# Output products and means of the linear attention, one step of the softmax later

## Chip, cores and metric

The kernel runs on one core of a Trainium2 chip. The metric is the device time of one execution in microseconds (us), lower is better; 3 runs of the kernel before are given.

## What is computed

One layer of a hybrid decoder: a SwiGLU block (FFN), a mixer, a second SwiGLU block, for 512 tokens of width 1024 in float32. The mixer has two branches. The first is a causal softmax attention with forget gates, 8 heads of width 64, whose queries come in blocks of 128. The second is a gated linear attention, 4 heads in chunks of 64 tokens:

```python
attn = where(tril, q_in @ k_in.T, 0)      # inside a chunk
state[n+1] = decay[n] * state[n] + k_st[n].T @ v[n]
o = attn @ v + q_in @ state               # "o" below
o = o * rsqrt(mean(o*o) + eps) * gain     # the mean is "ms" below
```

Then both branches are projected, gated, summed and projected once more.

## The kernel before

All engines run hand-written programs in a fixed order, joined by semaphores. A float32 product is made of three matmuls on high and low parts (lines 1601 to 1609), so TensorE (PE) has most of the work.

The part around the change is a loop over 38 steps, sl = 0 to 37, which each engine writes out in its own order: ScalarE (ACT) from line 905, VectorE (DVE) from 1472, TensorE from 1863. Steps 0 to 31 each start one softmax block: head sl // 4, query block sl % 4, so that its width is 128, 256, 384 or 512 keys for sl % 4 = 0 to 3. In one step:

- TensorE makes the scores of block sl (lines 1876 to 1878) after a wait for the exponentials of block sl - 2 (its count is sl - 1, line 1869). It then runs some blocks of input projection that fill the step (line 1883, called "filling" here): 3, 3, 2 and 0 blocks of three matmuls for sl % 4 = 0 to 3 from step 16 on (line 324). Then come the pieces of the linear attention that `gla_slots` gives to the step, then the transposes of the probabilities of block sl - 2 (line 1949), and in each fourth step, sl % 4 = 3, the product with the values of one head (line 1959).
- DVE takes the maximum of block sl (line 1476), the reciprocal of its sum (1480), work on a finished filling unit, the low part of the transposed probabilities of block sl - 2 (1494), in some steps sums of a head (1500) or the low part of a pair of heads (1505), and then the linear attention's pieces: the chain of states (1516, 1519), a gated product (1538), the scaled output (1543) and the low part of the squares (1545). Last, in some steps, the low part of a weight unit (1041).
- ACT takes the exponentials of block sl (912), the high part of the transposed probabilities (940), a sum of a head (946) or a pair's high part (950), the linear attention's copies and squares (968, 971, 975, 978), and the scaling of the probabilities (981).

The pieces of the linear attention are numbered: 0 and 1 transposes of keys, 2 and 3 the chunk scores of heads 0 and 1, 4 and 5 the key-value products of this pair ("kv"; piece 5 also holds DVE's chain of seven states), 6 the output product o of head 0, 7 its mean ms, 8 and 9 the same of head 1; 10 to 17 repeat 2 to 9 for heads 2 and 3. An ms product waits for the high and low parts of the squares (line 1938), which ACT (line 975) and DVE (line 1545) make of the output product in the step in which that product stands. Each piece alternates between two PSUM banks and waits for the reader of the piece two before it (line 1899).

```python
if sl >= 2:
    pe.wait_ge(exp_done, sl - 1)
...
if kind == "ms":
    pe.wait_ge(sq_lo_out, n + 1)
    mm(dst, mean_g[:, :], sq_hi, start=True, stop=False)
```

After the loop ACT makes the logarithm and the exponential of all means (lines 991 and 993, step 36), DVE and ACT finish the branch's output, and TensorE goes on with the gate projections (line 1968).

Of the kernel before, what the change touches and what calls it, by code (L numbers as in the profile page):

```python
# [108 lines left out]
def macaron_layer(nc, h_store, x_t, g1cols, x, w1g, w1u, w1d, g1post, gmpre, w_in, b_forget, w_alpha, b_alpha,  # L109
                  gla_g, w_bf, w_bg, w_out, gmpost, g2pre, w2g, w2u, w2d, g2post, out):  # L110
    with ExitStack() as ctx:
# [200 lines left out]
        def gain(g):  # L312
            return g.rearrange("(o n) -> o n", o=1).to_broadcast([P, D])


        gla_slots = {14: (0,), 16: (1,), 17: (2, 3), 18: (4, 5), 20: (6,), 22: (7, 8), 24: (9, 10), 25: (11, 12),
                     26: (13,), 28: (14,), 30: (15, 16), 32: (17,)}
        gated_slots = {25: 0, 29: 1, 33: 2, 37: 3}
        SLOTS_B = NS + 6

# [1816 lines left out]
```

## Time and profile before

| | us |
|---|---|
| median of 3 runs | 1080.15 |
| lowest, highest | 1079.99, 1081.3 |
| the profiled execution | 1081.57 |
| its span, first to last instruction | 1079.8 |
| its TensorE busy | 1067.4 |
| its VectorE, ScalarE busy | 721.7, 528.1 |

The mean granted clock of TensorE was 0.999 of full speed. Times in the trace are microseconds from the start of the span. A row of the timeline gives start, duration, engine, line, operation, operands and count of merged instructions; in square brackets stands how long the engine sat idle before and what released it. A matmul's duration includes the pipeline's latency, so successive matmuls overlap in it: the distance from one start to the next is what one costs.

### The profile page before, as it was taken

How to read it: one execution, taken by the hardware profiler on the slowest of the kernel's cores; microseconds unless marked ns; L12 is line 12 of the kernel's file. 1: busy time of each engine (PE TensorE's matmuls, PEld its weight loads, DVE VectorE, ACT ScalarE, POOL GpSimd, SP SyncE). 2: the span in 40 equal slices, each digit the busy share in tenths (PEclk: the TensorE clock that was granted, in tenths of full speed). 3: DMA queues.
4: the chain of work that ended last, by engine and by line, in shares of the span. 5: the costliest groups of instructions: out<-in, count | busy, mean ns of one | idle time of the engine just before them, and what ended most of it. 6: DMA issues, size and time to landing. Idle time of an engine off the chain costs nothing.

```text
span 1079.8 us, 16040 instructions
## 1 busy us (share of the span) xinstructions
PE 1067.4 (99%) x6490; PEld 951.6 (88%) x6490; DVE 721.7 (67%) x870; ACT 528.1 (49%) x765; POOL 44.6 (4%) x96
## 2 busy tenths in 40 slices
PE   8999999999999999999999999999999999999997
PEld 6899999998888978888888888889899999998886
DVE  6788998889535663476664333458778888789334
ACT  7354555557324573667773222344445455466222
POOL 2000000000001210001000000011000000000001
PEclk9999999999999999999999999999999999999999
DMA  9522422421721544333115335315524224313512
GB/s 301 186 79 79 150 86 79 155 81 40 260 79 54 176 124 108 84 78 80 40 40 156 97 97 172 100 39 176 156 79 149 87 79 154 121 39 105 207 39 79
DMA packets 118134, 121.20 MB, mean 112 GB/s; under 512 B 6544, under 2 KB 100768, under 8 KB 118064
## 3 DMA queue, kind: packets, MB, share of 16 engines
q1 hardware_dynamic: 113744, 113.37, 33.8%
q10 hardware_dynamic: 3344, 4.20, 1.4%
q0 software_dynamic: 976, 2.66, 0.7%
q8 instruction: 48, 0.79, 0.3%
q14 instruction: 22, 0.18, 0.1%
HBM read 111.80 MB, written 6.29 MB: 109 GB/s over the span
## 4 chain that ended last, share of the span: by engine, by line
PE 91%; DVE 3%; ACT 3%; issue 1%; DMA 1%; POOL 0%; ACTq 0%; DVEq 0%; POOLq 0%
PE bank L1616 17%; PE bank L1702 11%; PE bank L1704 11%; PE bank L1703 11%; PE bank L1606 7%; PE bank L1608 7%; PE bank L1607 7%; PE bank L1764 2%; PE bank L1765 2%; PE bank L1766 2%; PE bank L1852 1%; PE bank L1853 1%; PE bank L1854 1%; PE bank L1671 1%; PE bank L1672 1%
## 5 line engine op out<-in xcount | busy, mean ns | idle before, releaser
L1702 PE MATMUL bank<-tc,w_hi 128*128 128x256 f32 x576 | 163.0, 283 | 0.0
L1703 PE MATMUL bank<-tc,w_hi 128*128 128x256 f32 x576 | 163.0, 283 | 0.0
L1704 PE MATMUL bank<-tc,w_lo 128*128 128x256 f32 x576 | 163.0, 283 | 0.0
L1041 DVE TENSOR_TENSOR w_lo<-raw,w_hi 128x1024 fp32r<-128x1024 f32 x71 | 86.6, 1221 | 96.4 <-ACT w_hi L603 96.3
L1606 PE MATMUL bank<-u_hi,w_hi 128*128 128x512 f32 x312 | 123.9, 397 | 0.2 <-issue 0.2
L1702 PE MATMUL bank<-u_hi,w_hi 128*128 128x256 f32 x432 | 122.4, 283 | 0.8 <-DVE scr L1236 0.8
L1704 PE MATMUL bank<-u_hi,w_lo 128*128 128x256 f32 x432 | 122.3, 283 | 0.0
L1703 PE MATMUL bank<-u_lo,w_hi 128*128 128x256 f32 x432 | 122.3, 283 | 0.0
L1608 PE MATMUL bank<-u_hi,w_lo 128*128 128x512 f32 x312 | 121.7, 390 | 0.0
L1607 PE MATMUL bank<-u_lo,w_hi 128*128 128x512 f32 x312 | 121.6, 390 | 0.0
L1702 PEld LDWEIGHTS bank<-tc,w_hi 128*128 128x128 f32 x576 | 110.6, 192 | 0.0
L1703 PEld LDWEIGHTS bank<-tc,w_hi 128*128 128x128 f32 x576 | 110.6, 192 | 0.0
L1704 PEld LDWEIGHTS bank<-tc,w_lo 128*128 128x128 f32 x576 | 110.6, 192 | 0.0
L603 ACT ACTIVATE w_hi<-raw 128x1024 fp32r<-128x1024 f32 x71 | 74.7, 1054 | 55.9 <-PE bank L1608 24.3
L1616 PE MATMUL bank<-w_hi,a_hi 128*128 128x512 f32 x280 | 86.6, 391 | 0.0
L1616 PE MATMUL bank<-w_lo,a_hi 128*128 128x512 f32 x280 | 86.2, 389 | 0.0
L1616 PE MATMUL bank<-w_hi,a_lo 128*128 128x512 f32 x280 | 86.2, 389 | 0.0
L1702 PEld LDWEIGHTS bank<-u_hi,w_hi 128*128 128x128 f32 x432 | 82.9, 192 | 1.1 <-DVE scr L1236 1.0
L1703 PEld LDWEIGHTS bank<-u_lo,w_hi 128*128 128x128 f32 x432 | 82.9, 192 | 0.1
L1704 PEld LDWEIGHTS bank<-u_hi,w_lo 128*128 128x128 f32 x432 | 82.9, 192 | 0.0
L1223 DVE TENSOR_TENSOR w_lo<-raw,w_hi 128x1024 fp32r<-128x1024 f32 x28 | 34.3, 1224 | 72.3 <-ACT w_hi L709 72.2
L1147 DVE TENSOR_TENSOR w_lo<-raw,w_hi 128x1024 fp32r<-128x1024 f32 x54 | 66.0, 1222 | 23.6 <-ACT w_hi L675 23.6
(272 smaller groups left out, 2243.7 us busy)
## 6 DMA issues: line engine op xcount, KB each, us to landing
raw<-in_w_in SPq DMA_DIRECT2D x40, 512.0 KB, 3.8
raw<-in_ffn_w_down SPq DMA_DIRECT2D x34, 512.0 KB, 4.3
h<-in_ffn_w_gate SPq DMA_DIRECT2D x9, 1024.0 KB, 5.4
h<-in_ffn_w_up SPq DMA_DIRECT2D x9, 1024.0 KB, 9.1
raw<-in_ffn_w_gate SPq DMA_DIRECT2D x9, 1024.0 KB, 5.4
raw<-in_ffn_w_up SPq DMA_DIRECT2D x9, 1024.0 KB, 8.0
h_store<-h SPq DMA_DIRECT2D x2, 2048.0 KB, 9.4
h<-h_store SPq DMA_DIRECT2D x2, 2048.0 KB, 9.2
```

Of the source, the lines that this page charges most:

```text
L603: nc.scalar.activation(w_hi[:, slot(u), :], raw[:, slot(u), :], ACT.Copy).then_inc(hi_ready, 1)
L1041: V.tensor_tensor(w_lo[:, slot(u), :], raw[:, slot(u), :], w_hi[:, slot(u), :].bitcast(F32), ALU.subtract).then_inc(lo_ready, 1)
L1147: V.tensor_tensor(w_slot(w_lo, u), w_source(layer, q, n), w_slot(w_hi, u).bitcast(F32), ALU.subtract).then_inc(lo_ready, 1)
L1223: V.tensor_tensor(w_lo[:, slot(u), :], raw_down(layer, n), w_hi[:, slot(u), :].bitcast(F32), ALU.subtract).then_inc(lo_ready, 1)
L1606: mm(dst, w_hi[:, slot(u), w], rhs_hi[:, k - k0, :], start=k == k0, stop=False)
L1607: mm(dst, w_hi[:, slot(u), w], rhs_lo[:, k - k0, :], start=False, stop=False)
L1608: last = mm(dst, w_lo[:, slot(u), w], rhs_hi[:, k - k0, :], start=False, stop=k == k1)
L1616: last = mm(bank[:, 2 * t + c, :], a[:, s, toks], w[:, s, c * HALF:(c + 1) * HALF], start=first and a is a_hi and w is w_hi, stop=final an ...
L1702: mm(dst, w_hi[:, slot(u), w], moving(n, 0, k), start=first and k == 0, stop=False, skip_group_check=True)
L1703: mm(dst, w_hi[:, slot(u), w], moving(n, 1, k), start=False, stop=False, skip_group_check=True)
L1704: last = mm(dst, w_lo[:, slot(u), w], moving(n, 0, k), start=False, stop=k == KD // 2 - 1, skip_group_check=True)
L1764: mm(dst, a_hi[:, s, toks], w_hi[:, s, cols], start=start, stop=False, skip_group_check=True)
```

## The change

In `gla_slots` the output products and means are put one step later: piece 6 (o of head 0) from step 20 to 21, pieces 7 and 8 (ms of head 0, o of head 1) from 22 to 23, piece 14 from 28 to 29, pieces 15 and 16 from 30 to 31, piece 17 from 32 to 33. Piece 9 (ms of head 1) stays in step 24, as do the chunk scores and key-value products of heads 2 and 3. ACT, DVE and TensorE all read this table, so all of a piece moves with it on each of them. No instruction is added or taken away.

```diff
-        gla_slots = {14: (0,), 16: (1,), 17: (2, 3), 18: (4, 5), 20: (6,), 22: (7, 8), 24: (9, 10), 25: (11, 12),
-                     26: (13,), 28: (14,), 30: (15, 16), 32: (17,)}
+        gla_slots = {14: (0,), 16: (1,), 17: (2, 3), 18: (4, 5), 21: (6,), 23: (7, 8), 24: (9, 10), 25: (11, 12),
+                     26: (13,), 29: (14,), 31: (15, 16), 33: (17,)}
         gated_slots = {25: 0, 29: 1, 33: 2, 37: 3}
```

## Rows read from the trace of the kernel before

**Rows 1.** The page's first part: busy time of each engine, share of the span, instructions.

```profile
PE 1067.4 (99%) x6490; PEld 951.6 (88%) x6490; DVE 721.7 (67%) x870; ACT 528.1 (49%) x765; POOL 44.6 (4%) x96
```

**Rows 2.** TensorE's waits over the span: line, releaser, total, times, longest.

```profile
PE bank L1876 <- DMA a_lo<-qk: 1.0, 1, 1.0
```

**Rows 3.** Timeline of TensorE, end of step 20 and start of step 21.

```profile
501.11 0.39 PE L1608 MATMUL bank<-u_hi,w_lo 128*128 128x512 f32 x1
501.91 1.13 PE L1930 MATMUL bank<-scr,arena 128*128 128x128 f32 x8 [0.41 <-DVE scr L1519]
...
504.67 0.55 PE L1949 MATMUL bank<-ident,scr 128*128 128x128 f32 x3
504.98 0.36 PE L1876 MATMUL bank<-qk 128*128 128x256 f32 x1
...
505.36 0.45 PE L1606 MATMUL bank<-u_hi,w_hi 128*128 128x512 f32 x1
```

**Rows 4.** Timeline of DVE, step 18's chain of states and step 19's maximum.

```profile
499.50 2.27 DVE L1519 SCALAR_TENSOR_TENSOR scr<-scr,decay,bank 128x128 f32<-128x128 f32 x6
501.68 0.68 DVE L1476 TENSOR_REDUCE neg_max<-bank 128x1 f32<-128x512 f32 x1
```

**Rows 5.** Timeline of ACT: end of step 19's exponentials, step 21's high part.

```profile
502.99 0.19 ACT L912 ACTIVATION_READ_ACCUMULATOR scr<-bank,neg_max 128x1 f32 x1
...
509.67 0.59 ACT L940 ACTIVATE pt<-bank 128x512 fp32r<-128x512 f32 x1
```

**Rows 6.** Timeline of TensorE, steps 21 to 24.

```profile
507.48 0.60 PE L1949 MATMUL bank<-ident,scr 128*128 128x128 f32 x4
507.84 0.42 PE L1876 MATMUL bank<-qk 128*128 128x384 f32 x1
...
509.77 0.39 PE L1939 MATMUL bank<-a_hi,mean_g 128*128 128x512 f32 x1
...
512.91 0.33 PE L1949 MATMUL bank<-ident,scr 128*128 128x128 f32 x1
513.00 0.48 PE L1876 MATMUL bank<-qk 128*128 128x512 f32 x1
...
513.60 0.38 PE L1949 MATMUL bank<-ident,scr 128*128 128x128 f32 x2
...
515.05 0.27 PE L1876 MATMUL bank<-qk 128*128 128x128 f32 x1
```

**Rows 7.** Timeline of DVE, steps 20 to 22.

```profile
507.49 0.75 DVE L1543 TENSOR_SCALAR arena<-bank,gn 128x512 f32<-128x512 f32 x1
508.15 0.68 DVE L1545 TENSOR_TENSOR a_lo<-scr,a_hi 128x512 fp32r<-128x512 f32 x1
...
510.29 0.69 DVE L1494 TENSOR_TENSOR pt<-bank,pt 128x512 fp32r<-128x512 f32 x1 [0.33 <-ACT pt L940]
510.90 0.68 DVE L1505 TENSOR_TENSOR a_lo<-scr,a_hi 128x512 fp32r<-128x512 f32 x1
511.50 0.55 DVE L1476 TENSOR_REDUCE neg_max<-bank 128x1 f32<-128x384 f32 x1
```

**Rows 8.** Timeline of TensorE, step 28: the output product of head 2.

```profile
531.99 1.12 PE L1930 MATMUL bank<-scr,arena 128*128 128x128 f32 x8
```

**Rows 9.** Timeline of ACT, step 27: end of the exponentials.

```profile
533.06 0.19 ACT L912 ACTIVATION_READ_ACCUMULATOR scr<-bank,neg_max 128x1 f32 x1
```

**Rows 10.** Timeline of DVE, step 29: the gated product.

```profile
541.58 0.68 DVE L1538 TENSOR_TENSOR arena<-arena 128x512 f32<-128x512 f32 x1
```

**Rows 11.** Timeline of TensorE: at the kernel's start, and behind the wait in step 16.

```profile
10.89 1.05 PE L1808 MATMUL bank<-u_hi,w_lo 128*128 128x512 f32 x2
11.74 1.05 PE L1811 MATMUL bank<-u_lo,w_hi 128*128 128x512 f32 x2
...
485.87 0.44 PE L1606 MATMUL bank<-u_hi,w_hi 128*128 128x512 f32 x1
...
488.00 0.60 PE L1905 MATMUL bank<-ident,arena 128*128 128x128 f32 x4
```

## The prediction

> **What bounds the kernel.** I read the page first. TensorE is busy 99% of the span, DVE 67% [rows 1], so the end is set by TensorE wherever it does not wait, and a moved piece is worth only what it does to TensorE's waits. The list of TensorE's waits came next: in the softmax loop there are just two that it shows, 1.0 us for a DMA in step 16 [rows 2] and one before the first output product in step 20, shown as 0.41 us idle [rows 3]. Last I read the timelines of TensorE, DVE and ACT side by side over steps 18 to 36. The reader is to see two things in them. In step 20 TensorE reaches the output product before DVE has ended its chain of states. And behind that chain, in DVE's order, stands the maximum of softmax block 19 [rows 4], which TensorE needs (by way of ACT's exponentials) before the scores of block 21. So far that second lateness is hidden: the output product lies between.
>
> **Part 1, the wait that goes (step 20).** The last filling matmul starts at 501.11; such matmuls follow each other every 0.23 us (9 of them between 505.36 and 507.48 [rows 3, 6]), so the output product could start at 501.34. It starts at 501.91 [rows 3]. The change takes this away: -0.57 us. It is more than the 0.41 that the row calls idle, because a matmul's modelled end overlaps its successor.
>
> **Part 2, the wait that takes its place (step 21).** Without the product, step 20's three transposes start at 501.34 and take 504.98 - 504.67 = 0.31 us [rows 3]: TensorE stands before the scores of block 21 at 501.65. These wait for the exponentials of block 19. Nothing that leads to them moves: DVE's chain of states runs from 499.50 to 501.77, the maximum to 502.36 [rows 4], and ACT ends the exponentials with their sum at 502.99 + 0.19 = 503.18 [rows 5]. From a DVE end to the matmul it releases the trace shows 501.77 to 501.91 [rows 3, 4]; I take 0.12 for the hand-over, so the scores start at 503.30. Wait: +1.65 us. Bounds: 1.55 with no hand-over at all, 1.7 with 0.17. Before, the 2.8 us output product covered this, and TensorE came at 504.98, 1.8 us after the exponentials.
>
> **Part 3, the mean in step 23.** Times go on from 503.30. Scores and filling of step 21 take 507.48 - 504.98 = 2.50 [rows 3, 6] to 505.80. The output product takes 512.91 - 509.77 less 0.46 for the two mean matmuls (at 0.23), that is 2.68 [rows 6], to 508.48. Its consumers then stand late in both queues, behind the transposed probabilities of block 19: in the step's order TensorE makes the four transposes after the output product, they are done 0.60 later [rows 6], 509.08, and DVE and ACT deal with them before they touch the output. ACT's high part takes 0.59 [rows 5], to about 509.71, and DVE's low part starts at 509.74. Then DVE in its order, by distances of starts [rows 7]: low part 0.61, low part of a pair of heads 0.60, scaled output 0.66, low part of the squares 0.68 to its end: 512.29. (ACT's pair, square and high part end before DVE asks for them.) TensorE meanwhile: transposes 0.36, scores and filling of step 22 509.77 - 507.84 = 1.93, one transpose 0.09, scores of block 23 0.60 [rows 6]: 508.48 + 2.98 = 511.46. The mean waits from 511.46 to about 512.40: +0.94 us. In the kernel before it had the filling of step 22 and a whole step to itself as cover. Bounds: 0.5 if the hand-overs overlap better than in these rows, 1.4 if ACT comes late too.
>
> The mean of head 1 stays in step 24 while its output product moves to the end of step 23. Step 23 has no filling, so the product ends only some 0.6 us later relative to it, but ACT and DVE are later too. By the same distances the low part of its squares ends near 519.2, and TensorE, which starts step 24 at 515.05 + 1.94 = 516.99 and needs 0.33 for the scores and 2.1 for the filling, arrives at 519.4. I cost it at nothing; the cover is 0.2 us thin, and if it is gone it costs up to 0.5.
>
> **Part 4, the same in the second pair of heads.** In step 28 TensorE's filling ends at 531.99 [rows 8]; no wait is gained here. Three transposes (0.31) bring it to 532.30, the exponentials of block 27 end at 533.06 + 0.19 = 533.25 [rows 9], so the scores of block 29 start at 533.37: +1.07 us (0.95 to 1.15). From there the pattern of part 3 repeats, 511.46 - 503.30 = 8.16 to the mean and 9.10 to its release, but in step 29 DVE also has the gated product ahead of the output, 0.68 long and 0.6 to the next start [rows 10]. So the mean in step 31 waits 0.94 + 0.6 = +1.54 us (1.0 to 2.0). The mean of head 3 goes to step 33 and has two steps' time: nothing.
>
> **What else moves.** All else on the path keeps its distance from TensorE. SP's queue and POOL's have no moved instruction: POOL's masks follow ACT's copies of the chunk scores, which stay; SP's weight loads follow DVE's low parts with several units in hand. ACT's key and query spreads for the last pair of heads are issued in step 19 or 20, ahead of everything moved. The final logarithm starts after the last head's product, so the tail, with its short wait at its end, shifts as a whole. ACT and DVE get some 1.3 us free in steps 20, 22 and 28, but TensorE has no further wait there that this could shorten.
>
> **A rule about the clock.** Behind the 1.0 us wait in step 16 nine filling matmuls take 488.00 - 485.87 = 2.13, 0.24 each [rows 2, 11]: full clock, the upper level of 2.4 GHz. At the start of the kernel, where TensorE had sat idle for most of the time, two take 0.85, 0.43 each [rows 11]: the lower level, 1.2 GHz. The new waits of 1 to 1.65 us are longer than the one observed, so a fall can't be excluded by the row. The Trainium skill, page "TensorE: Matmul & The Clock Gate", section "HAM oscillation — how this bites in real kernels", warns that gaps between bursts drop the array to half clock; no run here has shown one in this stage. By the row the sum has nothing for it; by that rule each wait could add some us, which is a rival below.
>
> **Sum.** -0.57 + 1.65 + 0.94 + 1.07 + 1.54 = +4.6 us. The rows come from an execution of 1081.57 us (span 1079.8 and 1.8 around it), 1.4 above the median of 1080.15 and inside what the three runs differ by plus a little. The difference is set against the median: 1080.15 + 4.6 = 1084.75, given as 1084.7. About 0.2%, 2.2 us, is what a measurement of this kernel can tell from no change.
>
> **Rivals.**
>
> (a) Only the waits for the exponentials come, the means are covered: -0.57 + 1.65 + 1.07 = +2.15, 1082.3 us. For it: ACT and DVE were relieved of 1.3 us just before, and hand-overs are where my distances are weakest. Against it: DVE's chain in part 3 begins with transposes that TensorE itself issues after the product, so the relief doesn't help. 0.12, about half of it inside 0.2%.
>
> (b) Not slower: the change does just what its words suggest, the wait of step 20 goes and the product is fully covered, -0.57, 1079.6 us. This decides at one place: the exponentials of block 19 would have to end before 501.65, which they would if DVE's chain of states ended 1.5 us sooner. With everything freed in step 20 standing behind it in DVE's order, I see nothing that makes it so. 0.07.
>
> (c) Dearer: the thin cover in step 24 gives way (0.5), the late ACT and DVE work reaches the transposes that need the scaled probabilities or the next scores (0.5 to 1 in each pair of heads), +6.6, 1086.8 us. 0.10.
>
> (d) The clock falls behind a wait. If 12 filling matmuls then ran at 0.43 in place of 0.23 us, this is 2.4 us more for one fall: +7, 1087.2 us. 0.03. This is what the rule of the page named above would give.
>
> That the change does not do what it says has no room here: the table is the order of the programs.
>
> **How the numbers follow.** Forecast 0.68, 1083.6 to 1085.8 by its own bounds. The range reaches from (a) to (c): 1082.2 to 1086.8, leaving out (b), (d) and edges. Slower by over 0.2%: the forecast, (c), (d) and part of (a), 0.86. Within 0.2%: (b) and the rest of (a), 0.13. Faster by over 0.2% needs 2.2 us of waits that the loop doesn't have: 0.01.
>
> **What would show it.** In TensorE's waits, line 1930 behind DVE's states is gone; line 1876 waits for ACT's exponentials in steps 21 and 29, some 1.6 and 1.0 us; line 1939 waits for DVE's line 1545 in steps 23 and 31, some 0.9 and 1.5. Step 24 starts about 1.9 us later than at 515.05 [rows 6], and the gate projections about 4.5 later. The work of every line keeps its count. I am wrong if line 1876 shows no wait (then b), if line 1939 shows none (a), or if the 0.23 spacing changes.

## Result and the profile after

| | before | after |
|---|---|---|
| median | 1080.24 us (4 runs) | 1085.20 us (4 runs) |
| lowest, highest | 1079.99, 1081.3 | 1084.84, 1085.49 |
| ratio, 95% interval | | 1.0045, 1.0032 to 1.0058 |
| profiled execution, span | 1081.57, 1079.8 | 1084.97, 1083.2 |

The change costs 4.96 us by the medians, 3.5 to 6.3 by the interval; 4.6 were forecast (1084.7 us). The two profiled executions differ by less, 3.4 us, because the one of before was slow at its start: its first scores load at 425.3, those of the kernel after at 423.8, and nothing up to there differs between the kernels. So distances inside the softmax loop are compared below, and no absolute times: the loop's stretch from the value product of step 19 to that of step 35 (line 1959) takes 552.13 - 497.59 = 54.54 us before and 555.52 - 496.08 = 59.44 us after, +4.90. All of the loss is there.

TensorE's waits in the kernel after (line, releaser, total, times, longest), from step 16 on; the last row shown is a wait behind the loop:

```profile
PE bank L1939 <- DVE a_lo L1545: 2.4, 2, 1.5
PE bank L1876 <- ACT scr L912: 2.2, 2, 1.4
...
PE bank L1876 <- DMA a_lo<-qk: 1.0, 1, 1.0
...
PE bank L1606 <- DVE og L1556: 0.3, 1, 0.3
```

The wait of line 1930 for DVE's states, which [rows 3] show, is gone. Two new kinds, two of each, have come, and the wait for the DMA [rows 2] and the last one are what they were. The timeline of TensorE shows where (steps 20 to 24, then 28 to 31):

```profile
499.85 0.49 PE L1949 MATMUL bank<-ident,scr 128*128 128x128 f32 x3
501.73 0.39 PE L1876 MATMUL bank<-qk 128*128 128x256 f32 x1 [1.39 <-ACT scr L912]
...
509.30 0.47 PE L1876 MATMUL bank<-qk 128*128 128x512 f32 x1
...
510.95 0.47 PE L1939 MATMUL bank<-a_hi,mean_g 128*128 128x512 f32 x1 [0.89 <-DVE a_lo L1545]
511.26 0.40 PE L1940 MATMUL bank<-a_lo,mean_g 128*128 128x512 f32 x1
...
515.68 0.28 PE L1876 MATMUL bank<-qk 128*128 128x128 f32 x1
...
518.15 0.40 PE L1939 MATMUL bank<-a_hi,mean_g 128*128 128x512 f32 x1
...
532.65 0.49 PE L1949 MATMUL bank<-ident,scr 128*128 128x128 f32 x3
533.96 0.39 PE L1876 MATMUL bank<-qk 128*128 128x256 f32 x1 [0.82 <-ACT scr L912]
...
541.53 0.47 PE L1876 MATMUL bank<-qk 128*128 128x512 f32 x1
...
543.79 0.47 PE L1939 MATMUL bank<-a_hi,mean_g 128*128 128x512 f32 x1 [1.49 <-DVE a_lo L1545]
```

The reader is to see that the transposes of step 20 now start right behind the filling and that TensorE then stands before the scores of block 21. DVE shows why, in steps 18 to 19 as in [rows 4], and in step 21 as in [rows 7]. The second row here is ACT's, the end of the exponentials of block 19:

```profile
500.18 0.68 DVE L1476 TENSOR_REDUCE neg_max<-bank 128x1 f32<-128x512 f32 x1
...
501.48 0.19 ACT L912 ACTIVATION_READ_ACCUMULATOR scr<-bank,neg_max 128x1 f32 x1
...
508.25 0.69 DVE L1494 TENSOR_TENSOR pt<-bank,pt 128x512 fp32r<-128x512 f32 x1 [1.06 <-ACT pt L940]
508.86 0.68 DVE L1505 TENSOR_TENSOR a_lo<-scr,a_hi 128x512 fp32r<-128x512 f32 x1
509.46 0.75 DVE L1543 TENSOR_SCALAR arena<-bank,gn 128x512 f32<-128x512 f32 x1
510.12 0.68 DVE L1545 TENSOR_TENSOR a_lo<-scr,a_hi 128x512 fp32r<-128x512 f32 x1
```

The maximum of block 19 sits at 500.18, which is 501.68 [rows 4] less the 1.5 us of the start: it has not moved, TensorE has. The exponentials end at 501.67, and the scores of block 21 start 0.06 us later. In step 21 DVE idles 1.06 us until the transposed probabilities, which TensorE makes only behind the output product, and then works through four operations; the mean starts 0.15 us after the last of them ends.

### The profile page after: what moved, and what is told of

Its sections match the earlier page's. It is cut to its first block, busy times and chain, and to the rows that moved or that the text cites. A ratio compares the mean times of both kernels' runs of the same rounds, so it can differ in the third digit from the quotient of the medians.

```text
span 1083.2 us, 16040 instructions
## 1 busy us (share of the span) xinstructions
PE 1066.1 (98%) x6490; PEld 949.5 (88%) x6490; DVE 722.2 (67%) x870; ACT 527.6 (49%) x765; POOL 44.6 (4%) x96
## 4 chain that ended last, share of the span: by engine, by line
PE 89%; DVE 4%; ACT 3%; issue 2%; DMA 1%; POOL 0%; SPq 0%; ACTq 0%; DVEq 0%; POOLq 0%
PE bank L1616 17%; PE bank L1702 11%; PE bank L1704 11%; PE bank L1703 11%; PE bank L1606 7%; PE bank L1608 7%; PE bank L1607 7%; PE bank L1764 2%; PE bank L1765 2%; PE bank L1766 2%; PE bank L1852 1%; PE bank L1853 1%; PE bank L1854 1%; PE bank L1671 1%; PE bank L1672 1%
```

## The experiments

The loop's stretch is from the value product of step 19 to that of step 35 in the profiled execution of each kernel. Medians stand against the kernel before on the same chip. A stretch belongs to one execution: those of e4_outputs_late and e8_before_chain_early are from executions among the longest of their kernel, in which the granted clock fell for a while (see there), and that of e5_chain_early is from the shortest of its four, 1084.85 to 1088.25 us.

The edits move lines. In e5_chain_early, e6_max_first and e8_before_chain_early the chain of states has the lines 1488 and 1491 in place of 1516 and 1519, and DVE's lines between its new and its old place stand 15 higher (the reciprocal 1495, the low part of the transposed probabilities 1509). In e7_both_mended, e9_squares_first and e10_all_first all of TensorE's lines stand 16 higher. The text keeps the numbers of the kernel after; the rows have their own.

| kernel | median, its runs | ratio, 95% interval | stretch | against 54.54 |
|---|---|---|---|---|
| after | 1085.20 (4) | 1.0045, 1.0032 to 1.0058 | 59.44 | +4.90 |
| e1_first_pair | 1082.55 (10) | 1.0019, 1.0010 to 1.0029 | 56.76 | +2.22 |
| e2_second_pair | 1083.58 (7) | 1.0028, 1.0017 to 1.0040 | 57.31 | +2.77 |
| e3_means_late | 1081.65 (10) | 1.0011, 1.0001 to 1.0020 | 55.69 | +1.15 |
| e4_outputs_late | 1087.95 (4) | 1.0064, 1.0047 to 1.0081 | 62.23 | +7.69 |
| e5_chain_early | 1086.41 (4) | 1.0055, 1.0040 to 1.0071 | 59.69 | +5.15 |
| e6_max_first | 1082.56 (10) | 1.0017, 1.0008 to 1.0027 | 56.72 | +2.18 |
| e7_both_mended | 1079.93 (11) | 0.9994, 0.9985 to 1.0003 | 54.28 | -0.26 |
| e8_before_chain_early | 1083.01 (11) | 1.0024, 1.0015 to 1.0033 | 58.38 | +3.84 |
| e9_squares_first | 1082.84 (10) | 1.0020, 1.0011 to 1.0030 | 56.64 | +2.10 |
| e10_all_first | 1080.12 (11) | 0.9997, 0.9988 to 1.0006 | 53.95 | -0.59 |

### One pair of heads at a time

```diff
# e1_first_pair, against before
-        gla_slots = {..., 20: (6,), 22: (7, 8), ...
+        gla_slots = {..., 21: (6,), 23: (7, 8), ...
# e2_second_pair, against before
-                     26: (13,), 28: (14,), 30: (15, 16), 32: (17,)}
+                     26: (13,), 29: (14,), 31: (15, 16), 33: (17,)}
```

> Only the first pair of heads is moved (pieces 6 to 8), the second stays as in the kernel before. My theory (two new waits in each pair, one for the exponentials because DVE's chain of states stands ahead of the softmax maximum, one of the mean for the low part of its squares): the trace of the changed kernel gives for this pair -0.57 + 1.57 + 1.05 us and 0.1 for restarts, +2.1 us against the kernel before, about 1082.3 us; waits of line 1876 for ACT once and of line 1939 for DVE once, steps 28 on without any. Rival, that the loss is one that only builds up over both pairs (ACT and DVE getting later and later): clearly less than 2.1, and the rest with the second pair.

> Only the second pair of heads is moved (pieces 14 to 17). My theory: +1.00 for the exponentials of block 27, +1.66 for the mean in step 31, 0.1 for restarts, +2.8 us, about 1083.0 us, while the 0.57 wait in step 20 stays (line 1930 behind DVE's states). With the first pair's +2.1 it adds up to the 4.9 of the changed kernel. Rival (built up over both): clearly less than 2.8.

Both came out as my theory had it: +2.22 and +2.77 in the stretch where 2.1 and 2.8 were expected, 4.99 together against the 4.90 of the whole change, with one of each kind of wait in the trace of each. By the medians, 1082.55 and 1083.58 against 1080.46 of before, it is +2.1 and +3.1. Each pair carries its own two waits; nothing builds up from the first to the second.

### Only the means late, only the outputs late

```diff
# e3_means_late: outputs 6 and 14 stay
+        gla_slots = {..., 20: (6,), 23: (7, 8), ...
+                     26: (13,), 28: (14,), 31: (15, 16), 33: (17,)}
# e4_outputs_late: 7, 8 and 15, 16 stay
+        gla_slots = {..., 21: (6,), 22: (7, 8), ...
+                     26: (13,), 29: (14,), 30: (15, 16), 33: (17,)}
```

> The first output product of each pair stays in step 20 or 28; the mean and the second output product go to 23 or 31, the last mean to 33, as in the change. My theory: moving these costs nothing, since the output product in step 20 or 28 still covers the exponentials and the mean has two steps' cover. 1080.2 us, within 0.3 of before, the 0.57 wait in step 20 stays, and at most 0.1 us before the scores of block 23, whose exponentials end just as TensorE gets there. Rival, that emptying steps 22 and 30 and filling 23 and 31 (steps with no filling) is itself what makes TensorE wait: +2 us or more.

> Only output products 6 and 14 move (to 21 and 29), with the last mean to 33; mean and second output stay in 22 and 30. My theory: the waits for the exponentials are the same (1.57 and 1.00), the wait of step 20 is gone, and the mean waits are longer by what TensorE no longer does ahead of them (the scores of block 23 or 31 and a transpose, 0.69): 1.05 + 0.69 = 1.74 and 1.66 + 0.69 = 2.35. Sum -0.57 + 1.57 + 1.00 + 1.74 + 2.35 + 0.2 for restarts = +6.3 us, 1086.4 us. Rival, that the mean waits come from step 23 and 31 having no filling: +2 us only, 1082.2 us.

With the outputs in their old places line 1876 waits for ACT no more and the wait of line 1930 is back, as expected. But moving the means and second outputs is not free: +1.15 us. The timeline of all engines of this kernel in step 24, with the one new wait:

```profile
514.34 0.45 PE L1606 MATMUL bank<-u_hi,w_hi 128*128 128x512 f32 x1
...
514.60 0.60 ACT L978 ACTIVATE scr<-bank 128x512 f32<-128x512 f32 x1
...
515.08 0.61 ACT L971 ACTIVATE scr<-bank 128x512 f32<-128x512 f32 x1
...
515.72 0.75 DVE L1543 TENSOR_SCALAR arena<-bank,gn 128x512 f32<-128x512 f32 x1 [0.55 <-ACT scr L971]
...
516.38 0.69 DVE L1545 TENSOR_TENSOR a_lo<-scr,a_hi 128x512 fp32r<-128x512 f32 x1
...
517.22 0.47 PE L1939 MATMUL bank<-a_hi,mean_g 128*128 128x512 f32 x1 [0.58 <-DVE a_lo L1545]
```

The filling that starts at 514.34 ends its turn at 516.45 (nine matmuls, 2.1 us), the mean of head 1 starts at 517.22: +0.77. Another 0.15 lies ahead of the scores of block 23, where I had given at most 0.1. This is the thin cover of step 24 that the prediction named and costed at nothing, and at up to 0.5 if it were gone. Here it gives way, because TensorE has no wait in steps 21 and 23 and comes to step 24 sooner, 17.7 us after the value product of step 19 (514.00 - 496.32) against 19.6 in the changed kernel; ACT takes the square (line 971) only behind the exponentials, a high part and the copy of the first mean. In the changed kernel the low part of the squares ends at 517.44 and TensorE comes at 518.15. So the waits aren't terms that can be added up freely: the earlier ones pay for the later one.

For e4_outputs_late the two mean waits were to grow to 1.74 and 2.35 us, and they did, to 1.7 and 2.3 by the starts of the matmuls (1.51 and 2.12 idle as the trace counts it). Yet the stretch is 7.69 longer, not 6.3. Its times stood in two groups, 1086.49 and 1086.64, and 1089.26 and 1089.39; the profiled one is of the upper. What it has more goes with the granted clock (a window's busy time of PE, PEld, DVE, ACT, POOL, then the clock, DMA share, GB/s):

```profile
543.00:545.00 2.00, 0.77 (x4) 0.29 (x2) 2.00 (x4) 1.59 (x4) 0.00 (x0) 1.00 0.00 0
545.00:547.00 2.00, 1.12 (x3) 0.95 (x4) 1.26 (x4) 0.76 (x3) 0.00 (x0) 0.69 0.04 8
547.00:549.00 2.00, 2.00 (x11) 1.77 (x9) 0.79 (x2) 0.40 (x1) 0.00 (x0) 0.50 0.00 0
549.00:551.00 2.00, 2.00 (x16) 1.92 (x16) 0.00 (x0) 0.01 (x1) 0.00 (x0) 0.95 0.00 0
```

```profile
545.88 0.77 PE L1939 MATMUL bank<-a_hi,mean_g 128*128 128x512 f32 x1 [2.12 <-DVE a_lo L1545]
...
550.63 0.33 PE L1949 MATMUL bank<-ident,scr 128*128 128x128 f32 x1
```

Right behind this wait of 2.3 us the clock is at half, 1.2 GHz, for some microseconds. Mean and output product take 550.63 - 545.88 = 4.75 us there and 547.02 - 543.79 = 3.23 in the changed kernel, at 2.4 GHz: 1.5 us, about the excess of 1.4. A second execution of the same kernel:

> The kernel with only the output products moved, once more. Its times stood in two groups, 1086.5 and 1089.3 us, and its profiled execution (1089.3) had the granted clock at 0.83 in the 10 us in which the wait of 2.1 us lies. If the clock's fall behind that wait is what parts the groups, an execution of the lower group has a granted clock of 1.00 there and the sum of the waits, about +6.3; if not, the lower group has less waiting.

It gave 1089.5 and 1086.9 us. The profiled execution was again the upper one, with waits of 2.11, the clock again at 0.83 over the ten microseconds from 540 and a stretch of 62.28. No execution of the lower group has been profiled, so that the clock parts the groups is not shown; shown is only that the upper group has the fall. The mean granted clock of the unprofiled executions points the same way: 0.998 and 0.999 in the lower group against 0.997 twice in the upper, 0.998 against 0.997 in the second run, where 1.5 us lost in 1088 make 0.001. But the kernel before varies by more than that on the same two chips, 0.997 to 1.0. The fall alone can't be the 2.8 us between the groups. Both profiled executions also start late: their first scores load at 425.3 and 425.5, as in the profile of before, and at 423.8 in that of the changed kernel. Together that would be 3.0 us, if the lower group starts early, which no trace shows.

### What the wait for the exponentials hangs on

```diff
# e5_chain_early (on after), e8_before_chain_early (on before): DVE
                     V.tensor_reduce(neg_max[:, sl:sl + 1], ..., negate=True).then_inc(max_ready, 1)
+                for g in gla_slots.get(sl, ()):
+                    ...
+                    if kind == "kv" and n % 2:
+                        ...    # the chain of states, moved up from behind line 1505
# e6_max_first (on after): the same place, one step later
+                for g in gla_slots.get(sl - 1, ()):
+                    ...
```

> The changed kernel, with DVE's chain of states of each pair put earlier in its own step (18 and 26), right behind the softmax maximum. The same DVE work still stands ahead of the maximum of block 19 and 27. My theory (the maximum waits for DVE's turn, whatever the work is): the waits before the scores of blocks 21 and 29 get only so much shorter as DVE idles less, 0.5 and 0.7 us, to about 1.1 and 0.3; 1084.0 us. Rival, that the chain's own end is what matters (the output product's data): both waits gone, -2.6, 1082.6 us.

> The changed kernel, with DVE's chain of states put one step later, behind the maximum of block 19 or 27. My theory: line 1876 no longer waits for ACT, -1.57 - 1.00, the mean waits of line 1939 (1.05 and 1.66) stay as they are, since they count from TensorE's own transposes; 1082.6 us. Rival, that the late chain now delays the output product in step 21 or the scaled probabilities: less than 1 us gained.

e6_max_first did what my theory had it do: 1082.56 against the 1082.6 expected. DVE in step 19 of it, and TensorE's wait for DVE over the loop:

```profile
497.49 0.68 DVE L1476 TENSOR_REDUCE neg_max<-bank 128x1 f32<-128x512 f32 x1
...
498.40 2.26 DVE L1491 SCALAR_TENSOR_TENSOR scr<-scr,decay,bank 128x128 f32<-128x128 f32 x6
```

```profile
PE bank L1939 <- DVE a_lo L1545: 2.4, 2, 1.5
```

Line 1876 has no wait for ACT any more, line 1939 waits 0.89 and 1.49 as in the changed kernel, to the hundredth. That the maximum stands behind the chain in DVE's order is thus the cause of 4.90 - 2.18 = 2.7 of the 4.9 us.

e5_chain_early came out wrong for both theories: 1086.4, where 1084.0 and 1082.6 were expected. Both waits for ACT vanish, but only because TensorE stands still earlier, before the filling of steps 20 and 28. It is best seen in the kernel in which nothing else is changed:

> The kernel before, with DVE's chain of states earlier in its own step (behind the maximum of block 18 and 26). My theory: the chain ends some 2 us sooner, the wait of 0.57 us before the output product in step 20 is gone, the reciprocal that is now behind the chain is needed late enough: 1079.7 us, 0.5 under before, too little to be told from the times, so the trace must show it (no wait of line 1930). Rival: the late reciprocal delays the scaled probabilities and gives the gain back or more, 1081 us.

1083.0 against the 1079.7 expected and the 1081 of the rival. TensorE's waits in its loop:

```profile
PE bank L1606 <- DVE qk L1425: 1.7, 1, 1.7
PE bank L1876 <- DMA a_lo<-qk: 0.9, 1, 0.9
PE bank L1606 <- DVE arena L1504: 0.9, 1, 0.9
```

and DVE in step 18 of it:

```profile
496.94 0.29 DVE L1488 COPY scr<-bank 128x128 f32<-128x128 f32 x1 [1.38 <-PE bank L1921]
497.26 2.27 DVE L1491 SCALAR_TENSOR_TENSOR scr<-scr,decay,bank 128x128 f32<-128x128 f32 x6
499.45 0.16 DVE L1495 RECIPROCAL rinv<-rowsum 128x1 f32<-128x1 f32 x1
499.64 1.41 DVE L1425 SCALAR_TENSOR_TENSOR qk<-bank,qk 64x512 fp32r<-64x512 f32 x2
501.07 0.29 DVE L1509 TENSOR_TENSOR pt<-bank,pt 128x128 fp32r<-128x128 f32 x1
```

(The chain is the rows of lines 1488 and 1491, the reciprocal 1495.) The wait of step 20 for the states is gone, as I expected, but I had looked only at the reciprocal that is put behind the chain. The low part of the queries (line 1425), which stands behind it too, frees the PSUM bank into which the filling of step 20 goes (the wait of line 1882). It now ends at 501.05, and the filling waits for it. My expectation missed that second consumer, a bank that TensorE waits for: the same kind of miss that makes such a change look free. This execution too has a fall of the clock, shown below, which took 1.3 us; without it the stretch would be some 2.5 us longer than before, an estimate from 3.84 - 1.3, and the medians differ by 2.47. Further executions of the same kernel:

> The kernel before with the chain of states early in its own step, once more. Times of 1082.3 to 1084.0 and 1085.3 to 1085.8 us; its profiled execution (1085.5) had the granted clock at 0.83 behind the wait of 1.7 us in step 20. If the clock is what parts the groups, an execution near 1082.5 has 1.00 there and the same waits.

Five runs, 1082.47 to 1084.78; the profiled one, 1084.78, again has half clock behind the 1.74 us wait, and a stretch of 58.43. Its two longest executions, 1084.53 and 1084.78, have a mean granted clock of 0.996, the three others 0.998 to 0.999; of these there is no profile here either. But e5_chain_early has the same wait, 1.72 us at the same place, in an execution in which the clock stays up; up to that wait the two kernels have the same programs. Side by side, first e8_before_chain_early, then e5_chain_early (columns as above):

```profile
499.00:501.00 2.00, 0.47 (x5) 0.33 (x3) 1.90 (x5) 1.36 (x2) 0.00 (x0) 1.00 0.00 0
501.00:503.00 2.00, 1.81 (x6) 1.47 (x7) 1.10 (x4) 1.20 (x4) 0.00 (x0) 0.70 0.03 8
503.00:505.00 2.00, 2.00 (x7) 1.62 (x6) 1.76 (x3) 0.85 (x3) 0.00 (x0) 0.50 0.36 83
505.00:507.00 2.00, 2.00 (x18) 1.88 (x16) 0.16 (x1) 0.34 (x2) 0.00 (x0) 0.94 0.73 152
```

```profile
499.00:501.00 2.00, 1.78 (x8) 1.51 (x9) 1.12 (x4) 1.20 (x4) 0.00 (x0) 1.00 0.00 0
501.00:503.00 2.00, 2.00 (x14) 1.69 (x13) 1.76 (x3) 0.86 (x3) 0.00 (x0) 1.00 0.36 83
503.00:505.00 2.00, 2.00 (x14) 1.79 (x12) 1.34 (x3) 1.62 (x5) 0.00 (x0) 1.00 0.72 155
```

So one and the same wait may or may not cost the clock.

### The wait of the mean, and both mended

```diff
# e9_squares_first (on after): ACT and DVE, outputs of heads 0 and 2
+                for g in gla_slots.get(sl, ()):
+                    ...
+                    if kind == "o" and n % 2 == 0:
+                        ...    # square and its high part (DVE: scaled output, low part)
                 if 2 <= sl < NS + 2:
                     s = sl - 2
                     act.wait_ge(pt_ready, s + 1)
```

e7_both_mended is e6_max_first with this edit, e10_all_first the same for all four outputs.

> The changed kernel, in which ACT and DVE take the output product of steps 21 and 29 ahead of the transposed probabilities; the chain of states stays where it was. My theory (the mean waits count from the transposes that stand behind the output product): line 1939 waits no more, -1.05 - 1.66, and the waits for the exponentials stay, 1.57 and 1.00; +2.2 us against before, about 1082.6 us. Rival, that the mean waits are only the exponentials' waits seen a second time: less than 1 us gained on the changed kernel.

> As the one before (maximum first), and ACT and DVE take the output product of steps 21 and 29 (square, its high part, scaled output, low part) ahead of the transposed probabilities. My theory: the squares' low part then ends near 2.2 us after the output product, where TensorE needs about 3.0 to come to the mean, so line 1939 doesn't wait either and nothing of the four new waits is left, while the wait of step 20 is gone too: 0.5 us under the kernel before, 1079.7 us. Rival: the transposed probabilities, now 1.3 us later on ACT and DVE, make TensorE wait elsewhere, 1081 us or more.

> The kernel with both causes mended, and now in steps 23 and 31 too ACT and DVE take the output product ahead of the transposed probabilities. In the trace of the mended kernel the mean of head 1 in step 24 still started some 0.3 us later than the filling before it ended. My theory: ACT's square there comes 0.7 us sooner, this last wait goes, and from the value product of step 19 to that of step 35 the kernel needs 0.5 to 0.6 us less than the kernel before (54.54); 0.5 us under it in time, about 1079.8 us, at the edge of what the runs can tell. Rival: later transposed probabilities give it back, nothing gained on the mended kernel.

e9_squares_first: 1082.84 where 1082.6 was expected. Line 1939 waits for DVE no more, and line 1876 waits 1.36 and 0.82 where the changed kernel has 1.39 and 0.82:

```profile
PE bank L1892 <- ACT scr L912: 2.2, 2, 1.4
```

Together with e6_max_first this takes the two causes apart: either can be removed without touching the other, and each is worth 2.7 to 2.8 us of the stretch.

With both mended the table of the change costs nothing: the stretch is 0.26 us shorter than that of before, 0.59 with all outputs taken first, about the 0.57 of the wait in step 20 that the change does remove. For e7_both_mended I had expected the whole 0.5; what is missing is the mean in step 24, which starts 0.24 us late (515.30 against 514.83 + 0.23) and costs a restart, and which is gone in e10_all_first. In that last kernel TensorE's timeline has no wait between steps 17 and 36. The times say the same within what they can tell: 1079.93 against 1080.54, and 1080.12 against 1080.43, both with intervals that hold 1. A gain on the kernel before is shown by the traces alone, not by the times.

## Why the prediction was right

Point by point, by its own steps; the measured values are from the rows of the kernel after.

| part | forecast | measured | worked out |
|---|---|---|---|
| 1, wait of step 20 gone | -0.57 | -0.57 | line 1930 waits no more |
| 2, exponentials of block 19 | +1.65 | +1.57 | 501.73 - (499.85 + 0.31) |
| 3, mean in step 23 | +0.94 | +1.05 | 510.95 - (509.30 + 0.60) |
| 3, mean in step 24 | 0 | 0 | 518.15, filling's turn ends at 515.68 + 0.33 + 2.12 = 518.13 |
| 4, exponentials of block 27 | +1.07 | +1.00 | 533.96 - (532.65 + 0.31) |
| 4, mean in step 31 | +1.54 | +1.66 | 543.79 - (541.53 + 0.60) |
| sum | +4.6 | +4.71 | |

What is left to the 4.90 of the stretch, 0.19, is mostly a term that the prediction lacked: behind a wait the first matmul of a mean takes longer until the next starts, 511.26 - 510.95 = 0.31 at both means, against 518.39 - 518.15 = 0.24 at the mean that doesn't wait. The two exponential waits were put 0.08 and 0.07 too high, mostly by the hand-over (0.12 assumed, 0.06 measured at the first), the two mean waits 0.11 and 0.12 too low. These errors cancel in part, and that is luck; so is that the medians came within 0.5 us of each other, as the start alone moves an execution by 1.5 us. Each term was built from the starts of neighbouring rows, which hold the overlap of successive instructions in them, and not from their durations; that none is off by more than 0.12 I put down to this.

The step that carried the forecast was to ask of the 2.8 us output product not what it waits for but what it hides: the lateness of ACT's exponentials. [rows 3] and [rows 4] were enough for that, and e6_max_first shows it by changing DVE's order alone. The second step, that the squares are late because their consumers stand behind transposes that TensorE issues later, is shown by e9_squares_first. Of the signs that the prediction named, step 24 came 19.60 - 17.46 = 2.14 us later by distances from the value product of step 19, where 1.9 was forecast; its chain took 2.68 us for the first output product too, which lasts 504.67 - 501.91 = 2.76 in [rows 3], and lacked the restarts.

Rival (a), means covered, is out by the two waits of line 1939; rival (b), not slower, by the waits of line 1876; rival (c), dearer, did not come: the thin cover of step 24 held, with 0.7 us rather than 0.2. Rival (d), the fall of the clock, did not come in the changed kernel, whose granted clock is 1.00 around all four waits, of at most 1.66 us. It came in two experiments with longer waits, of 1.9 and 2.3 us (see below), at 1.3 and 1.5 us for a fall where 2.4 were put; whether its 0.03 was too low is not shown. The rows at the kernel's start [rows 11] carry less than was read from them: their spacing of 0.43 us is that of the rows with a granted clock of 0.50 in e8_before_chain_early, but the profile's granted clock for 8:12 us reads 1.00, and TensorE had been busy for 4.8 of the first 8 us, not idle for most of them.

That what ACT and DVE get free in steps 20 and 28 shortens no wait was right too. What I had wrong in the expectations of the experiments was of one kind: in e3_means_late, e5_chain_early and e8_before_chain_early I counted only the next waiter, and the cost came from one further on.

## What to carry to other kernels

Before work is moved on the engine that bounds a kernel, look up what that work hides: list for the instruction right behind its old place when its inputs are ready, and compare with the time at which the engine would now get there. In programs that run in order, a consumer is only as early as whatever stands ahead of it on each engine between, so check where in DVE's and ACT's order the consumers stand, and what frees the banks. Moving a piece to remove a short wait pays only if the order on the other engines is changed with it; here that made the difference between +4.9 us and -0.3 to -0.6 us in the loop's stretch, at a table that was the same; the times can't tell the latter from nothing.

## What the runs showed of the hardware

The granted clock of TensorE fell to 0.50, its level of 1.2 GHz, behind a single wait of 2.3 us (both profiles of e4_outputs_late) and behind one of 501.19 - 499.31 = 1.9 us (both profiles of e8_before_chain_early), with the engine busy before the wait and after it. The price was 1.5 us of slower matmuls in the one, and in the other 1.3 us in the nine filling matmuls alone, which took 504.62 - 501.19 = 3.43 us in place of 2.1. Behind the same wait in the one profile of e5_chain_early, and behind the waits of the changed kernel, of up to 1.66 us, the clock stayed at 1.00. The Trainium skill, page "TensorE: Matmul & The Clock Gate", section "HAM oscillation — how this bites in real kernels", has gaps between bursts halve the clock; these traces agree in kind, with one gap in otherwise dense work. What decides between fall and no fall at equal waits stays open. The four executions with the fall loaded their first scores at 424.6 to 425.5 us, that of e5_chain_early at 423.4; one case is too few to build on.

A wait on TensorE that the profile calls 0.41 or 1.49 us idle costs 0.57 or 1.66 in starts of matmuls, since a matmul's modelled end lies over its successor's start.
